# Residual turns of the out and down projection, from TensorE to VectorE's 32 x 32 blocks, in a hybrid decoder block on one core

## The chip, the cores and the metric

One Trainium2 chip, one of its cores. The metric is the device time of one execution in microseconds (us), taken over several runs. The profiled execution is one more run, with its own time; its span is the time from the first to the last instruction in the trace.

## What is computed

The block adds two residuals. The lines that matter here:

```python
h = jnp.concatenate([meta, x], axis=1)            # 16 meta tokens ahead of 256
...
m = (jax.nn.sigmoid(ga) * (y_h @ w_branch_hgrn[l])
     + jax.nn.sigmoid(gb) * (y_a @ w_branch_dsa[l]))
h = h + m @ w_out[l]                              # residual 1: x, 2048 channels
u = rmsnorm(h, ffn_norm_w[l])
a = causal_dwconv(u @ w_ffn_gate[l], ffn_conv_w[l], ffn_conv_b[l])
h = h + (jax.nn.silu(a) * (u @ w_ffn_up[l])) @ w_ffn_down[l]   # residual 2: h
return rmsnorm(h, final_norm_w)[:, N_META:]
```

x is float32, one sequence of 256 tokens, 2048 channels. The input x lies in memory with a token per row.

## The kernel before

Every weight matrix is cut into units of 128 columns, all 2048 rows (16 slices of 128). There are 256-column panels of raw float32 weights, two buffers, loaded by SyncE (`load`, L433); each panel waits for `lo_ready`, the low parts of the panel two before it. ScalarE rounds a unit to `w_hi` (L1136), VectorE makes the rest `w_lo` (L1447), both four units deep, and TensorE makes three products per slice: high by high, high by low, low by high. The order of the work on each engine is written out by hand, and engines meet at semaphores. `ahead(n)` on ScalarE and VectorE makes the high and low part of unit n + 3.

Through the gates, the merge (16 units from `U_MERGE`) and the out projection (16 units from `U_OUT`) activations lie turned: 128 channels on the partitions, tokens along the row. T is 272, TQ is 258: the last two meta tokens and the 256 of x. The unit n of the out projection gives channels 128n to 128n + 127 of h.

Residual 1. x has tokens on the rows, so TensorE turns it into the bank of the unit, ahead of the products (L1031: three turns of 128 x 128 a unit, one for the meta rows and two for x, with the identity), and the 48 products of the unit are summed on top. POOL fetches x for two units at a time into `x_st` (`x_panel`, L603 and L604), two buffers, the first two before its loop over the gates of the merge. VectorE then copies the bank to `h_res` (L1794, `out_free`), ScalarE makes the scaled and rounded `u2_hi` (L1385; the profile calls the place u_hi) and VectorE its rest `u2_lo` (L1796). TensorE may use one of the two banks (`ps[6]`, `ps[7]`) again when `out_free` tells that the unit two before has been copied. POOL sums the squares of h over the units (L626, L631). This stage is a loop of 4 x 4 units on all engines.

The feed-forward has two halves of 22 blocks of hidden channels (`FH`). Its first unit begins with eight slices, then TensorE sums the squares over the partitions (L1058 for the units up to 14, L1060 for the last), and ScalarE and VectorE make the root of it (`h_rs`).

Residual 2. The down projection gives tokens on the rows again. In half 0, `residual` (L1079) turns h back on TensorE, four turns of 128 x 128 ahead of each of the eight groups of sums (two chunks of columns, two halves of a chunk, two blocks of tokens), into the bank in which `down` sums the products (L1092 to L1095). VectorE copies the bank to `h_tok` (`add`, L1851), which has the place of `h_res`; in half 1 it adds (L1853).

## Time and profile before

| | |
|---|---|
| median of 3 runs | 1599.75 us (1599.56 to 1600.13) |
| profiled execution | 1599.79 us |
| its span | 1598.0 us |
| granted TensorE clock | 0.999 of full speed |
| TensorE busy | 1586.3 us, 99% of the span |
| VectorE busy | 972.0 us, 61% |
| ScalarE busy | 708.5 us, 44% |
| POOL busy | 116.0 us, 7% |
| moved by DMA | 290.36 MB, mean 182 GB/s |

The busy time is an average over all stages. A line number such as L1031 is a line of the kernel. "PE" is TensorE's matmul side, DVE is VectorE, ACT is ScalarE, SP is SyncE; "SPq" and "ACTq" are their queues of transfers. Matmuls are pipelined, so a row's duration is longer than the distance from one to the next; the starts tell the pace.

### The profile page before, as it was taken

The page shows a single profiled execution, that of the slowest core. Times are in us where ns is not written, and L with a number is a line of the kernel's source. Part 1 is how long each engine was busy: PE and PEld are TensorE (multiplying, and loading weights), DVE is VectorE, ACT ScalarE, POOL GpSimd, SP SyncE. Part 2 cuts the span into 40 slices and gives each one's busy share as a digit, 9 for nine tenths or more (in the row PEclk, how much of TensorE's full clock was granted, in tenths as well). Part 3 has the DMA queues.
Part 4 walks back from the last instruction along what each step waited for, and adds up shares of the span by engine and source line. Part 5 has one row for each costly group of instructions (what it writes and reads, how often), then busy time and mean ns, then how long its engine had stood idle before and what let it go on. Part 6 is the DMA issues. An engine that isn't in the chain of part 4 may idle for free.

```text
span 1598.0 us, 29335 instructions
## 1 busy us (share of the span) xinstructions
PE 1586.3 (99%) x12162; PEld 1527.7 (96%) x12162; DVE 972.0 (61%) x1126; ACT 708.5 (44%) x746; POOL 116.0 (7%) x165
## 2 busy tenths in 40 slices
PE   9999999999999999999999999999999999999998
PEld 8999999999999999999999999998889999999886
DVE  7655878853355566786656666665445666666453
ACT  6433554544443345654345455544333334334342
POOL 1000140000000002352220000000000000000000
PEclk9999999999999999999999999999999999999999
DMA  7755555555555553576555565645455555565551
GB/s 244 227 179 164 158 165 179 178 179 179 179 189 180 159 159 119 191 246 203 177 191 191 172 195 165 203 162 204 173 198 181 188 180 187 174 194 198 196 210 54
DMA packets 244998, 290.36 MB, mean 182 GB/s; under 512 B 5697, under 2 KB 231218, under 8 KB 244530
## 3 DMA queue, kind: packets, MB, share of 16 engines
q1 hardware_dynamic: 238146, 278.78, 53.4%
q0 software_dynamic: 2176, 6.34, 1.2%
q10 hardware_dynamic: 4608, 4.23, 0.8%
q8 instruction: 55, 0.90, 0.2%
q14 instruction: 13, 0.11, 0.0%
HBM read 283.02 MB, written 6.32 MB: 181 GB/s over the span
## 4 chain that ended last, share of the span: by engine, by line
PE 99%; DVE 0%; ACT 0%; DMA 0%; issue 0%; SPq 0%; DVEq 0%
PE ps L654 25%; PE ps L655 24%; PE ps L656 24%; PE ps L1092 5%; PE ps L1095 5%; PE ps L1094 5%; PE ps L1041 2%; PE ps L1039 2%; PE ps L1040 2%; PE ps L817 1%; PE ps L685 0%; PE ps L792 0%; PE ps L934 0%; PE ps L1031 0%; PE ps L827 0%; PE ps L1079 0%
## 5 line engine op out<-in xcount | busy, mean ns | idle before, releaser
L654 PE MATMUL ps<-u_hi,w_hi 128*128 128x258 f32 (+2 forms) x2936 | 839.1, 286 | 0.0
L655 PE MATMUL ps<-u_lo,w_hi 128*128 128x258 f32 (+2 forms) x2936 | 831.4, 283 | 0.0
L656 PE MATMUL ps<-u_hi,w_lo 128*128 128x258 f32 (+2 forms) x2936 | 831.1, 283 | 0.0
L1447 DVE TENSOR_TENSOR w_lo<-raw,w_hi 128x2048 fp32r<-128x2048 f32 x259 | 598.1, 2309 | 353.6 <-ACT w_hi L1136 353.1
L1136 ACT ACTIVATE w_hi<-raw 128x2048 fp32r<-128x2048 f32 x259 | 495.9, 1916 | 565.1 <-PE ps L656 393.4
L654 PEld LDWEIGHTS ps<-u_hi,w_hi 128*128 128x128 f32 x2936 | 554.0, 189 | 5.1 <-DVE z_qf L1560 2.5
L655 PEld LDWEIGHTS ps<-u_lo,w_hi 128*128 128x128 f32 x2936 | 554.0, 189 | 0.3
L656 PEld LDWEIGHTS ps<-u_hi,w_lo 128*128 128x128 f32 x2936 | 553.8, 189 | 0.0
L1092 PE MATMUL ps<-w_hi,hid_hi 128*128 128x512 f32 x352 | 137.8, 391 | 0.0
L1095 PE MATMUL ps<-w_lo,hid_hi 128*128 128x512 f32 x352 | 137.1, 389 | 0.0
L1094 PE MATMUL ps<-w_hi,hid_lo 128*128 128x512 f32 x352 | 137.0, 389 | 0.0
L1095 PEld LDWEIGHTS ps<-w_lo,hid_hi 128*128 128x128 f32 x352 | 66.1, 188 | 14.0
L1094 PEld LDWEIGHTS ps<-w_hi,hid_lo 128*128 128x128 f32 x352 | 66.1, 188 | 13.4
L1092 PEld LDWEIGHTS ps<-w_hi,hid_hi 128*128 128x128 f32 x352 | 66.1, 188 | 13.3
L1039 PE MATMUL ps<-m_hi,w_hi 128*128 128x258 f32 x256 | 73.7, 288 | 0.0
L1041 PE MATMUL ps<-m_hi,w_lo 128*128 128x258 f32 x256 | 72.7, 284 | 0.0
L1040 PE MATMUL ps<-m_lo,w_hi 128*128 128x258 f32 x256 | 72.3, 283 | 0.0
L1318 ACT ACTIVATE gate_st<-ps 128x258 f32<-128x258 f32 x32 | 12.4, 387 | 100.0 <-PE ps L656 100.0
L1040 PEld LDWEIGHTS ps<-m_lo,w_hi 128*128 128x128 f32 x256 | 48.6, 190 | 0.0
L1039 PEld LDWEIGHTS ps<-m_hi,w_hi 128*128 128x128 f32 x256 | 48.5, 189 | 0.0
L1041 PEld LDWEIGHTS ps<-m_hi,w_lo 128*128 128x128 f32 x256 | 48.4, 189 | 0.0
L1834 DVE TENSOR_TENSOR g_raw<-ps,h_rs 128x258 f32<-128x258 f32 x44 | 18.8, 428 | 39.6 <-PE ps L656 37.9
(299 smaller groups left out, 1307.4 us busy)
## 6 DMA issues: line engine op xcount, KB each, us to landing
raw<-in_w_in_dram SPq DMA_DIRECT2D x47, 2048.0 KB, 8.5
raw<-in_w_ffn_gate_dram SPq DMA_DIRECT2D x22, 2048.0 KB, 8.1
raw<-in_w_ffn_up_dram SPq DMA_DIRECT2D x22, 2048.0 KB, 8.1
raw<-in_w_ffn_down_dram SPq DMA_DIRECT2D x20, 2048.0 KB, 7.6
raw<-in_w_out_dram SPq DMA_DIRECT2D x8, 2048.0 KB, 8.9
raw<-in_w_branch_hgrn_dram SPq DMA_DIRECT2D x8, 1024.0 KB, 5.5
raw<-in_w_branch_dsa_dram SPq DMA_DIRECT2D x8, 1024.0 KB, 8.8
gate_spill<-gate_st ACTq DMA_DIRECT2D x32, 129.0 KB, 3.9
```

The costliest lines, as they stand in the source:

```text
L654: mm(acc, w_hi[s][:, k, :], mov_hi(k), start=(k == first), stop=False)
L655: mm(acc, w_hi[s][:, k, :], mov_lo(k), start=False, stop=False)
L656: ins = mm(acc, w_lo[s][:, k, :], mov_hi(k), start=False, stop=(k == last))
L1039: mm(acc, w_hi[n % 4][:, k, :], m_hi[:, k, :], start=False, stop=False, skip_group_check=True)
L1040: mm(acc, w_hi[n % 4][:, k, :], m_lo[:, k, :], start=False, stop=False, skip_group_check=True)
L1041: ins = mm(acc, w_lo[n % 4][:, k, :], m_hi[:, k, :], start=False, stop=(k == KT - 1), skip_group_check=True)
L1092: mm(acc, hid_hi[:, f, rows], down_hi[s][:, i, :], start=(f == 0 and half == 1), stop=False, skip_group_check=True)
L1094: mm(acc, hid_lo[:, f, rows], down_hi[s][:, i, :], start=False, stop=False, skip_group_check=True)
L1095: ins = mm(acc, hid_hi[:, f, rows], down_lo[s][:, i, :], start=False, stop=(f == FH - 1), skip_group_check=True)
L1136: activation(w_hi[m % 4][:], raw[(m // 2) % 2][:, :, P * (m % 2):P * (m % 2) + P], ACT.Copy)\
L1447: v.tensor_tensor(w_lo[m % 4][:], raw[(m // 2) % 2][:, :, P * (m % 2):P * (m % 2) + P], w_hi[m % 4][:].bitcast(F32), ALU.subtract).then_in ...
L1834: link(v.tensor_tensor(g[:], ps[4 * half + u][:, 0:TQ], h_rs[:], ALU.mult))
```

## The change

TensorE turns nothing in the two projections any more.

x now comes from memory already shuffled: `x_blocks` views it in blocks of 32 tokens by 32 channels, and POOL's `x_quad` moves the channels of four units with 16 transfers of 32 partitions x 8 blocks x 32 numbers (128 bytes a piece) into `x_sh`, two buffers. A turn of VectorE within blocks of 32 x 32 (L1811) then gives `xt` with channels on the partitions. The meta rows are fetched by four more transfers and turned once, for all units (`xm_sh`, `xm`). VectorE turns x for a unit before it waits for that unit's products, adds bank and `xt` instead of copying the bank, turns h into `h_sh` behind `u2_lo`, and ScalarE stores `h_sh` with four transfers of 128-byte pieces to `h_spill` in memory, one unit later. When all is stored, POOL reads h back with tokens on the rows into `h_tok`, two transfers of 1 MB, and half 0 of the down projection adds to it, as half 1 does. The start flags of the sums change with that. The stage is written out flat on VectorE, ScalarE and POOL, no longer a loop.

```diff
--- before.py
+++ after.py
@@ -188,7 +188,11 @@
 
         HRES = R[0] + 2 * FH * SEQ * 4
         h_res = at("h_res", HRES, [P, KT, TQ])
-        x_st = [at(f"x_st{a}", BIAS + 3072 * a, [P, 3, 256]) for a in range(2)]
+        x_sh = [at(f"x_sh{a}", (BIAS, R[4])[a], [P, 4, SEQ]) for a in range(2)]
+        xt = [at(f"xt{a}", BIAS + 4096 + 1024 * a, [P, SEQ]) for a in range(2)]
+        xm_sh = at("xm_sh", R[7] + 5184, [P, KT, 32])
+        xm = at("xm", R[4] + 4096, [P, KT, 32])
+        h_sh = [at(f"h_sh{a}", R[4] + 6144 + 1024 * a, [P, SEQ]) for a in range(4)]
         h_sq = at("h_sq", R[7] + 640, [P, TQ])
         ssq = at("ssq", R[7] + 1672, [P, TQ])
         h_rs = at("h_rs", R[7] + 2704, [P, TQ])
@@ -374,6 +385,9 @@
         bd_cols = w_branch_dsa[0].rearrange("(k p) n -> p k n", p=P)
         wd_rows = w_ffn_down[0].rearrange("(k p) n -> p k n", p=P)
         x_rows = x[0].rearrange("(t p) n -> p t n", p=P)
+        x_blocks = x[0].rearrange("(b j) (k a i) -> a j k b i", j=32, a=4, i=32)
+        meta_blocks = meta_tokens.rearrange("j (k a i) -> a j k i", a=4, i=32)
+        h_blocks = h_spill.rearrange("(b j) (k a i) -> a j k b i", j=32, a=4, i=32)
 
 
         N_PANELS = U_END // 2
@@ -599,17 +613,8 @@
             pool.wait_ge(x_rs_ready, 1)
             for n in range(4):
                 gate_pair(n, n)
-            def x_panel(slot, cols):
-                pool.dma_start(x_st[slot][:, 1:3, :], x_rows[:, :, cols]).then_inc(x_st_in[slot], 16)
-                pool.dma_start(x_st[slot][P - 2:P, 0, :], meta_tokens[T0:META, cols]).then_inc(x_st_in[slot], 16)
-
             for n in range(3):
                 scale_gates(n, 16)
-            pool.wait_ge(o_gated, HEADS)
-            steps.link(pool, pool.memset(ssq[:], 0.0))
-            for b in range(2):
-                steps.link(pool, pool.memset(x_st[b][:, 0, :], 0.0))
-                x_panel(b, slice(256 * b, 256 * b + 256))
             with pool.Fori(0, 3) as i:
                 for a in range(4):
                     pool.wait_ge(m_ready, 4 * i + (a + 1))
@@ -619,6 +624,12 @@
                     scale_gates((a + 3) % 4, 16 * i + (16 if a == 0 else 32))
             scale_gates(3, 64)
 
+
+            def x_quad(q):
+                for a in range(4):
+                    for k in range(4):
+                        pool.dma_start(x_sh[q % 2][32 * a:32 * a + 32, k, :].rearrange("j (b i) -> j b i", i=32),
+                                       x_blocks[a, :, 4 * q + k, :, :]).then_inc(x_sh_in[q % 2], 16)
 
             def squares(n, tile, last=False):
                 pool.wait_ge(out_free, n + 3)
@@ -630,18 +641,32 @@
                     steps.link(pool, ins)
                     steps.link(pool, pool.tensor_tensor(ssq[:], ssq[:], h_sq[:], ALU.add))
 
-            with pool.Fori(0, 3) as i:
-                steps.enter(i, 8)
-                for b in range(2):
-                    pool.wait_ge(xt_turned, 4 * i + (2 * b + 2))
-                    x_panel(b, ds(512 * i + (512 + 256 * b), 256))
-                    for a in range(2):
-                        squares(4 * i + (2 * b + a), ds(4 * i + (2 * b + a), 1))
-            steps.leave(3)
-            for n in range(12, 16):
+            pool.wait_ge(o_gated, HEADS)
+            steps.link(pool, pool.memset(ssq[:], 0.0))
+            pool.wait_ge(projected, U_MERGE)
+            pool.wait_ge(ya_ready, 9)
+            pool.memset(xm_sh[:], 0.0).then_inc(xm_zeroed, 1)
+            x_quad(0)
+            pool.wait_ge(xm_zeroed, 1)
+            for a in range(4):
+                pool.dma_start(xm_sh[32 * a:32 * a + 2, :, :], meta_blocks[a, T0:META, :, :]).then_inc(xm_in, 16)
+            pool.wait_ge(projected, U_OUT)
+            x_quad(1)
+            for n in range(16):
+                if n in (4, 8):
+                    pool.wait_ge(xt_turned, n)
+                    x_quad(n // 4 + 1)
                 if n == 15:
                     pool.tensor_copy(spare[:, 5:6], ssq[:, 0:1]).then_inc(ssq_ready, 1)
                 squares(n, slice(n, n + 1), n == 15)
+            pool.wait_ge(u2h_ready, 16)
+            pool.wait_ge(u2l_ready, 16)
+            for a in range(4):
+                pool.wait_ge(h_out[a], 4 * 64)
+            pool.wait_ge(ssq_ready, 2)
+            for c in range(2):
+                pool.dma_start(h_tok[c][:], h_spill[:, 1024 * c:1024 * c + 1024].rearrange("(t p) n -> p t n", p=P))\
+                    .then_inc(h_in, 16)
 
 
         @block.tensor
@@ -1023,23 +1048,13 @@
             with pe.Fori(0, 4) as i:
                 for u in range(4):
                     n = U_OUT + u
-                    if u % 2 == 0:
-                        pe.wait_ge(x_st_in[u // 2], 32 * i + 32)
                     pe.wait_ge(out_free, 4 * i + (u + 1))
-                    bank = ps[6 + u % 2]
-                    for t in range(3):
-                        ins = mm(bank[:, P * t:P * t + P], x_st[u // 2][:, t, P * (u % 2):P * (u % 2) + P], ident[:],
-                                 is_transpose=True, start=(t == 0), stop=False, skip_group_check=True)
-                    ins.then_inc(xt_turned, 1)
                     pe.wait_ge(lo_ready, 4 * i + (n + 1))
                     for k in range(KT):
                         if u == 0 and k >= 14:
                             pe.wait_ge(m_ready, k + 1)
-                        acc = bank[:, P - 2:P - 2 + TQ]
-                        mm(acc, w_hi[n % 4][:, k, :], m_hi[:, k, :], start=False, stop=False, skip_group_check=True)
-                        mm(acc, w_hi[n % 4][:, k, :], m_lo[:, k, :], start=False, stop=False, skip_group_check=True)
-                        ins = mm(acc, w_lo[n % 4][:, k, :], m_hi[:, k, :], start=False, stop=(k == KT - 1),
-                                 skip_group_check=True)
+                        ins = products(ps[6 + u % 2][:, 0:TQ], n % 4, (k,), lambda k: m_hi[:, k, :],
+                                       lambda k: m_lo[:, k, :])
                     ins.then_inc(projected, 1)
             for half, (u_ff, u_down) in enumerate(((U_FF, U_DOWN), (U_FF2, U_DOWN2))):
 
@@ -1073,23 +1088,14 @@
                         gate_up(u, range(KT))
 
 
-                def residual(c, u, t):
-
-                    for g in range(4):
-                        mm(ps[down_bank(0, c, u, t)][:, P * g:P * g + P],
-                           h_res[:, 8 * c + 2 * g + u, 2 + P * t:2 + P * t + P], ident[:], is_transpose=True,
-                           start=(g == 0), stop=False, skip_group_check=True)
-
                 def down(j, t, half=half, u_down=u_down):
 
                     s = (u_down + j) % 4
                     for i in range(4):
                         c, f = down_at(j, i)
-                        if f == 0 and half == 0:
-                            residual(c, j % 2, t)
                         acc = ps[down_bank(half, c, j % 2, t)][:]
                         rows = slice(P * t, P * t + P)
-                        mm(acc, hid_hi[:, f, rows], down_hi[s][:, i, :], start=(f == 0 and half == 1), stop=False,
+                        mm(acc, hid_hi[:, f, rows], down_hi[s][:, i, :], start=(f == 0), stop=False,
                            skip_group_check=True)
                         mm(acc, hid_lo[:, f, rows], down_hi[s][:, i, :], start=False, stop=False, skip_group_check=True)
                         ins = mm(acc, hid_hi[:, f, rows], down_lo[s][:, i, :], start=False, stop=(f == FH - 1),
@@ -1380,14 +1386,21 @@
             loop(U_MERGE, 4, 4, merge_unit, early=1)
 
 
-            def out_unit(i, u, split):
-                act.wait_ge(out_free, 4 * i + (u + 3))
-                activation(u2_hi[:, ds(4 * i + u, 1), :].rearrange("p a t -> p (a t)"),
-                           h_res[:, ds(4 * i + u, 1), :].rearrange("p a t -> p (a t)"), ACT.Copy,
-                           scale=vec_a[:, ds(4 * i + (V_FFN + u), 1)]).then_inc(u2h_ready, 1)
-                split()
-
-            loop(U_OUT, 4, 4, out_unit, early=1)
+            def store_turned(u):
+                act.wait_ge(h_turned, u + 1)
+                for a in range(4):
+                    act.dma_start(h_blocks[a, :, u, :, :],
+                                  h_sh[u % 4][32 * a:32 * a + 32, :].rearrange("j (b i) -> j b i", i=32))\
+                        .then_inc(h_out[u % 4], 16)
+
+            for u in range(16):
+                act.wait_ge(out_free, u + 3)
+                activation(u2_hi[:, u, :], h_res[:, u, :], ACT.Copy, scale=vec_a[:, V_FFN + u:V_FFN + u + 1])\
+                    .then_inc(u2h_ready, 1)
+                ahead(U_OUT + u + 1)
+                if u:
+                    store_turned(u - 1)
+            store_turned(15)
             act.wait_ge(ssq_sum, 1)
             activation(h_rs[:], ps[4][:, 0:TQ], ACT.Sqrt, bias=eps[:], scale=1.0 / D).then_inc(h_std, 1)
 
@@ -1786,18 +1799,27 @@
                         .then_inc(m_ready, 1)
 
 
-            with dve.Fori(0, 4) as i:
-                for u in range(4):
-                    m = U_OUT + u
-                    dve.wait_ge(projected, 4 * i + (m + 1))
-                    h = h_res[:, ds(4 * i + u, 1), :].rearrange("p a t -> p (a t)")
-                    v.tensor_copy(h, ps[6 + u % 2][:, P - 2:P - 2 + TQ]).then_inc(out_free, 1)
-                    dve.wait_ge(u2h_ready, 4 * i + (u + 1))
-                    v.scalar_tensor_tensor(u2_lo[:, ds(4 * i + u, 1), :].rearrange("p a t -> p (a t)"), h,
-                                           vec_a[:, ds(4 * i + (V_FFN + u), 1)],
-                                           u2_hi[:, ds(4 * i + u, 1), :].rearrange("p a t -> p (a t)").bitcast(F32),
-                                           ALU.mult, ALU.subtract).then_inc(u2l_ready, 1)
-                    ahead(4 * i + (m + 1), m + 1)
+            for u in range(16):
+                m, h = U_OUT + u, h_res[:, u, :]
+                if u == 0:
+                    dve.wait_ge(xm_in, 64)
+                    v.transpose(xm[:].rearrange("p k t -> p (k t)"), xm_sh[:].rearrange("p k t -> p (k t)"))\
+                        .then_inc(xm_turned, 1)
+                    dve.wait_ge(xm_turned, 1)
+                if u % 4 == 0:
+                    dve.wait_ge(x_sh_in[(u // 4) % 2], 256 * (u // 8) + 256)
+                v.transpose(xt[u % 2][:], x_sh[(u // 4) % 2][:, u % 4, :]).then_inc(xt_turned, 1)
+                dve.wait_ge(xt_turned, u + 1)
+                dve.wait_ge(projected, m + 1)
+                v.tensor_tensor(h[:, 0:2], ps[6 + u % 2][:, 0:2], xm[:, u, 0:2], ALU.add)
+                v.tensor_tensor(h[:, 2:TQ], ps[6 + u % 2][:, 2:TQ], xt[u % 2][:], ALU.add).then_inc(out_free, 1)
+                dve.wait_ge(u2h_ready, u + 1)
+                v.scalar_tensor_tensor(u2_lo[:, u, :], h, vec_a[:, V_FFN + u:V_FFN + u + 1], u2_hi[:, u, :].bitcast(F32),
+                                       ALU.mult, ALU.subtract).then_inc(u2l_ready, 1)
+                if u >= 4:
+                    dve.wait_ge(h_out[u % 4], 64 * (u // 4))
+                v.transpose(h_sh[u % 4][:], h[:, 2:TQ]).then_inc(h_turned, 1)
+                ahead(m + 1, m + 1)
 
 
             dve.wait_ge(h_std, 1)
@@ -1820,6 +1842,9 @@
                     for u in range(4):
                         m = u_ff + u
                         if u == 3:
+                            if half == 0:
+                                for r in range(4):
+                                    dve.wait_ge(h_out[r], 4 * 64)
                             low(0)
                         if u >= 2:
                             c = conv[u - 2][:]
@@ -1843,14 +1868,14 @@
                     low(1)
                 steps.leave(FH // 2)
 
+                if half == 0:
+                    dve.wait_ge(h_in, 32)
+
                 def add(c, u, t, half=half):
 
                     h = chunk_cols(c, t, u)
                     bank = ps[down_bank(half, c, u, t)][:].rearrange("p (g c) -> p g c", c=P)
-                    if half == 0:
-                        v.tensor_copy(h, bank).then_inc(down_added, 1)
-                    else:
-                        v.tensor_tensor(h, bank, h, ALU.add).then_inc(down_added, 1)
+                    v.tensor_tensor(h, bank, h, ALU.add).then_inc(down_added, 1)
 
                 for j in range(1, FH - 3):
                     ahead(u_down + j, u_down + j)
```

POOL, at the end of its loop over the merge gates and into the out projection, before (x_st is the staged x, h_sq the squares, ssq their sum):

```order
L594 TENSOR_TENSOR gates_125<-gates_125,x_rs 128x516
L633 UNCONDITIONAL_BRANCH
L633 ISA
L603 ISA
L603 DMA x_st_127<-in_x_dram 128x2x256
L604 ISA
L604 DMA x_st_127<-in_meta_tokens_dram 2x256
L624 REGISTER_ALU
L626 ISA
L626 TENSOR_TENSOR h_sq<-h_res 128x258
```

The same place of POOL in the change:

```order
L608 TENSOR_TENSOR gates_125<-gates_125,x_rs 128x516
L645 MEMSET ssq 128x258
L648 MEMSET xm_sh 128x512
L631 DMA x_sh_127<-in_x_dram 32x8x32 x16
L652 DMA xm_sh<-in_meta_tokens_dram 2x16x32 x4
L631 DMA x_sh_128<-in_x_dram 32x8x32 x16
L637 TENSOR_TENSOR h_sq<-h_res 128x258
L642 TENSOR_TENSOR ssq<-ssq,h_sq 128x258
```

The first fetch of x has moved from ahead of the gate loop to behind it, and 36 transfers stand there where 2 stood; two more runs of 16 stand behind the squares of units 3 and 7.

VectorE, from the last unit of the merge into the first of the out projection, before:

```order
L1447 TENSOR_TENSOR w_lo_56<-raw_49,w_hi_52 128x2048
L1784 ISA
L1784 TENSOR_TENSOR m_lo<-gates_125,m_hi 128x258
...
L1794 COPY h_res<-ps 128x258
L1795 REGISTER_ALU
L1796 ISA
L1796 SCALAR_TENSOR_TENSOR u_lo<-h_res,vec_a,u_hi 128x258
L1446 REGISTER_ALU
L1447 TENSOR_TENSOR w_lo_57<-raw_50,w_hi_53 128x2048
```

And in the change:

```order
L1460 TENSOR_TENSOR w_lo_56<-raw_49,w_hi_52 128x2048
L1797 ISA
L1797 TENSOR_TENSOR m_lo<-gates_125,m_hi 128x258
...
L1806 STREAM_TRANSPOSE xm<-xm_sh 128x512
L1811 STREAM_TRANSPOSE xt_129<-x_sh_127 128x256
L1814 TENSOR_TENSOR h_res<-ps,xm 128x2
L1815 TENSOR_TENSOR h_res<-ps,xt_129 128x256
L1817 SCALAR_TENSOR_TENSOR u_lo<-h_res,vec_a,u_hi 128x258
L1821 STREAM_TRANSPOSE h_sh_133<-h_res 128x256
L1460 TENSOR_TENSOR w_lo_57<-raw_50,w_hi_53 128x2048
```

Two turns and a small add have come into each unit, one turn ahead of the wait for the products and one ahead of `w_lo`, and the turn of the meta rows once; the register work of the loop is gone.

## Rows read from the trace of the kernel before

**Rows 1.** The page: the chain that ended last, shares of the span by engine
```profile
PE 99%; DVE 0%; ACT 0%; DMA 0%; issue 0%; SPq 0%; DVEq 0%
```

**Rows 2.** TensorE's timeline between two out-projection units: start us, us, engine, line, op
```profile
780.40 0.28 PE L1041 MATMUL ps<-m_hi,w_lo 128*128 128x258 f32 x1
780.52 0.49 PE L1031 MATMUL ps<-ident,x_st 128*128 128x128 f32 x3
780.97 0.29 PE L1040 MATMUL ps<-m_lo,w_hi 128*128 128x258 f32 x1
```

**Rows 3.** Line L1031: its turns, ns min/median/max, first and last start
```profile
L1031 PE MATMUL ps<-ident,x_st x48: 270/272/273, 743.8 to 835.8; 128*128 128x128 f32 x48
```

**Rows 4.** Timeline of TensorE at the turns of h in the down projection
```profile
1157.90 0.40 PE L1095 MATMUL ps<-w_lo,hid_hi 128*128 128x512 f32 x1
...
1158.59 0.39 PE L1095 MATMUL ps<-w_lo,hid_hi 128*128 128x512 f32 x1
...
1159.72 0.40 PE L1095 MATMUL ps<-w_lo,hid_hi 128*128 128x512 f32 x1
```

**Rows 5.** Timeline of VectorE and ScalarE, one unit of the out projection
```profile
774.72 0.43 DVE L1794 COPY h_res<-ps 128x258 f32 x1 [0.82 <-PE ps L1041]
...
775.37 0.51 ACT L1385 ACTIVATE u_hi<-h_res,vec_a  x1 [3.80 <-DVE h_res L1794]
775.79 1.90 ACT L1136 ACTIVATE w_hi<-raw 128x2048 fp32r<-128x2048 f32 x1
...
777.73 2.66 DVE L1447 TENSOR_TENSOR w_lo<-raw,w_hi 128x2048 fp32r<-128x2048 f32 x1 [1.19 <-ACT w_hi L1136]
```

**Rows 6.** Groups of VectorE: line, op, count, busy us, mean ns, idle before
```profile
L1853 DVE TENSOR_TENSOR h_tok<-ps,h_tok 128x512 f32<-128x512 f32 x8 | 5.3, 687 | 12.6 <-PE ps L1095 12.6
...
L1804 DVE RECIPROCAL h_rs<-h_rs 128x258 f32<-128x258 f32 x1 | 1.8, 1759 | 0.0
```

**Rows 7.** Timeline of VectorE and ScalarE in code written out flat
```profile
652.88 0.77 DVE L1761 TENSOR_TENSOR z_v<-z_v,z_g 128x258 f32<-128x258 f32 x2 [1.37 <-ACT z_g L1364]
...
653.34 0.42 ACT L1367 ACTIVATE yh_hi<-z_v 128x258 fp32r<-128x258 f32 x1 [0.26 <-DVE z_v L1761]
```

**Rows 8.** A transfer's issue on ScalarE's queue, line L1320: ns min/median/max
```profile
L1320 ACTq DMA_DIRECT2D gate_spill<-gate_st x32: 338/338/383, 227.2 to 434.6; - x32
```

**Rows 9.** Timeline of VectorE and POOL ahead of the out projection
```profile
660.23 2.29 DVE L1447 TENSOR_TENSOR w_lo<-raw,w_hi 128x2048 fp32r<-128x2048 f32 x1 [1.38 <-ACT w_hi L1136]
...
660.88 0.76 POOL L603 DMA_DIRECT2D x_st<-in_x_dram  x1 [0.30 <-POOL x_st L611]
...
733.19 1.20 POOL L594 TENSOR_TENSOR gates<-gates,x_rs 128x516 f32<-128x516 f32 x1 [4.74 <-DMA gates<-gate_spill]
```

**Rows 10.** Lines L603 and L604, POOL's transfers: ns min/median/max, landing of L604
```profile
L603 POOL DMA_DIRECT2D x_st<-in_x_dram x8: 745/788/791, 659.0 to 812.3; - x8
...
L604 POOL DMA_DIRECT2D x_st<-in_meta_tokens_dram x8: 534/534/546, 659.7 to 813.1; - x8
...
DMA to landing us min/median/max: 2.6/5.9/7.0
```

**Rows 11.** DMA: out projection (share is 0.58), first 14 us, page's queues
```profile
743.80:841.50 97.70, 97.70 (x817) 97.70 (x816) 57.82 (x50) 37.02 (x32) 27.13 (x43) 1.00 0.58 186
...
DMA packets 3434, 3.91 MB, mean 279 GB/s; under 512 B 2150, under 2 KB 3162, under 8 KB 3162
...
q1 hardware_dynamic: 3434, 3.91, 86.2%
...
q1 hardware_dynamic: 238146, 278.78, 53.4%
...
q10 hardware_dynamic: 4608, 4.23, 0.8%
```

**Rows 12.** Timeline of POOL and TensorE at the sum of squares
```profile
842.55 0.62 POOL L626 TENSOR_TENSOR h_sq<-h_res 128x258 f32<-128x258 f32 x1 [4.39 <-DVE h_res L1794]
...
845.03 0.60 PE L1060 MATMUL ps<-h_sq,ones 128*128 128x258 f32 x2
```

More of the change, by code:

```diff
@@ L223, in hybrid_block @@
         gate_spill = nc.dram_tensor("gate_spill", (P, 2 * KT, TQ), F32).ap()
+        h_spill = nc.dram_tensor("h_spill", (SEQ, D), F32).ap()
         def sem(name):
@@ L339, in hybrid_block @@
         m_ready = sem("m_ready")
-        x_st_in = [sem("x_st_in0"), sem("x_st_in1")]
+        x_sh_in = [sem("x_sh_in0"), sem("x_sh_in1")]
+        xm_zeroed = sem("xm_zeroed")
+        xm_in = sem("xm_in")
+        xm_turned = sem("xm_turned")
         xt_turned = sem("xt_turned")
+        h_turned = sem("h_turned")
+        h_out = [sem(f"h_out{a}") for a in range(4)]
+        h_in = sem("h_in")
         ssq_ready = sem("ssq_ready")
```

## The prediction

> **What bounds the kernel now.** I read the page's chain of waits first: TensorE is 99% of the chain that ended last [rows 1]. So an edit pays only by what it takes off TensorE's instruction stream, and costs only by what makes TensorE wait. Two questions follow: how much do the 80 turns on TensorE (L1031, 48; L1079, 32) really take there, and does any new feeder become late. For the first I read TensorE's timeline around one turn of each kind [rows 2 to 4], for the second the loop that VectorE and ScalarE run beside each unit of the out projection [rows 5 to 8], POOL's queue [rows 9, 10] and the DMA engines [rows 11].
>
> **What leaves TensorE.** The busy time of a turn (272 ns [rows 3]) overstates it, since matmuls are pipelined; the starts tell. In the out projection a turn of three starts 0.12 us after the product before it, as any product does, but the second product behind it starts 0.45 us after the turn (780.52 to 780.97), where two products would start 0.12 apart: 0.33 us per unit [rows 2]. 16 units: **5.3 us**. In the down projection the third product of a group starts 1.13 us after the one before the turns (1158.59 to 1159.72), where three products behind each other take 0.69 us (1157.90 to 1158.59): 0.44 us per group of four, 8 groups: **3.5 us** [rows 4]. Nothing takes their place on TensorE, so 8.8 us is the most that can be won. The down part I take in full: its h is read back right behind the out projection, at about 850 us, and VectorE first adds it some 300 us later (at L1851's place), and the add that replaces the copy reads the same 512 columns from the bank, 0.69 us as in half 1 [rows 6]. The eight adds of half 0 cost nothing.
>
> **VectorE's loop in the out projection.** Before, a unit of TensorE lasts 6.12 us (15 units from 743.8 to 835.8, less the two turns between, 0.15) [rows 3]; after, 5.79. VectorE, ScalarE and VectorE form a ring per unit: copy of h, u_hi on ScalarE, w_hi on ScalarE, w_lo on VectorE, next copy [rows 5]. Its gaps: w_hi 0.42 behind u_hi, w_lo 1.94 behind w_hi, 2.29 for w_lo alone [rows 9]. From the copy's start to u_hi it is 0.65 in this looped code, but 0.46 in code written out flat (z_v 652.88, yh_hi 653.34) [rows 7], and the change writes this stage out flat. The change adds to the ring: the two-column add (258 columns cost 0.43 and 512 cost 0.69, so the fixed part is 0.17 at most; 0.1, as it runs behind another) and the turn of x ahead of the wait. No row shows a VectorE turn. Its lower bound is a copy of that width, 0.42 us; its upper the dearest row of that width, the reciprocal, 1.76 us; I take 0.42, since it too passes each column once, plus 0.05 for its own semaphore [rows 5, 6]. Ring: 0.1 + 0.46 + 0.42 + 1.94 + 2.29 + 0.47 = **5.7 us**, just under the 5.79 of TensorE. The second turn (h) fits in the 1.2 us for which VectorE waits for w_hi. ScalarE's four stores a unit are 4 x 0.34 = 1.4 us, beside 3.80 us that it idles before u_hi; what is queued behind them, the next u_hi, is not due before that [rows 5, 8].
>
> **The start of the stage.** VectorE now waits for the meta rows and the first x quad before it may free the first bank. POOL reaches them after its last gate product (733.19 + 1.20); two memsets, then 16 transfers at 0.79 (the nearest row: 256 pieces as well, 0.788) and 4 meta transfers at 0.55: 735.3 + 12.6 + 2.2 = 750.1. These landed 2.6 to 7.0 us after issue, 5.9 in the median, which I take: most of those eight had a weight load beside them, and so has this one [rows 9, 10]. Landed 756.0; turn of 512 columns 0.69, turn of x 0.47, adds 0.55: the first bank is free at 757.8. TensorE needs it at 743.8 + 2 x 5.79 = 755.4, and so waits **2.5 us**. From there VectorE is one unit further behind than before, and its ring (5.7) barely gains on TensorE (5.79).
>
> **The end of the stage.** The feed-forward begins with 24 products (0.12 each, 2.87 us), then a first product for the sum of squares (0.43 us from the one start to the other) and a second, for which POOL must have squared the last h (it ended at 843.17; L1060 starts at 845.03, so it was no wait) [rows 12]. After: TensorE could be there at 757.9 + 14 x 5.79 + 2.87 + 0.43 = 842.3. VectorE's last add ends at 757.8 + 15 x 5.68 = 843.0, POOL's square and a hop make 843.8. L1060 starts at 843.8, **1.2 us** earlier than before: of 5.3 us, 2.6 go at the start (the wait and a hop of 0.1) and 1.5 at the end. **Sum:** 1.2 + 3.5 = 4.7 us. The profiled execution took 1599.79, the median of the runs is 1599.75; 1599.8 - 4.7 = **1595.1 us**.
>
> **The small packets.** x and h now move in pieces of 128 bytes: three quads (12288) and the stores (16384) within the stage, 1792 packets per DMA engine. The engines are busy 0.58 of 97.7 us of the stage, 56.7 us; TensorE's 16 units are 92.6 us, so a packet may cost 20 ns before the engines are full. Bounds: in the first 14 us 3434 packets took 0.862 x 14 x 16 = 193 us; 2150 were under 512 bytes, and the other 3.25 MB at the kernel's mean (13.65 ms for 278.78 MB) are 159 us, leaving 16 ns for a small one. The upper end is the mean packet, 57 ns (1.2 KB), and the nearest store, 44 ns (q10: 0.8% of 16 x 1598 us for 4608 packets) [rows 11]. I take 16, as the nearest in size: 28.7 us, engines 92% full, and free of charge, though with little to spare.
>
> **Rivals.**
> 1. *No wait at the start* (meta lands in 2.6 us, the bank frees at 754.5): VectorE never limits TensorE and all 8.8 us stay: 1591.0. Against it: a weight load runs beside it. Chance 0.10.
> 2. *The ring is longer than a unit.* If the VectorE turn costs 0.8, or POOL's products catch w_lo (2.29 becomes 2.66 at 777.73, and in every second unit before [rows 5]), the ring is 5.9 to 6.1; each 0.1 us is 1.5 us at L1060. 1598 to 1603. Chance 0.13.
> 3. *The DMA engines fill up: slower.* Place: the 128-byte stores of ScalarE's queue beside the weight loads. It decides from 20 ns a packet. At 44 ns for a store the stage needs 56.7 + 12.3 + 45.1 = 114 us of every engine, 21.5 over the 92.6: 1599.8 - 8.8 + 21.5 = 1612.5; with 57 ns for all, 1657. For it: the margin is thin, and a late store also holds VectorE, which waits for the stores of four units ago before it turns h. Against it: the 16 ns above. Chance 0.17. The Trainium skill, "DMA: Bandwidth & Descriptors", Specifications, says that below 512 B the engine does read-modify-write; by that rule this case would hold, while the rows show small reads only and no small store.
> 4. *POOL's queue is late: slower.* Place: x_quad, 64 transfers in all. Each 0.1 us above 0.79 is 1.6 us at the start, and from 1.37 us a transfer quads 2 and 3 miss their units too. At 2 us: 1599.8 - 8.8 + 2.5 + 19.4 + 2 x 10 = 1633. For it: 16 in a row are in no row. Against: a transfer issued inside a w_lo (660.88 within 660.23 to 662.52) took its normal 0.76, w_lo its normal 2.29 [rows 9]. The Trainium skill, "SBUF — State Buffer", SBUF: two separate sides, warns that VectorE in a two-port mode locks GpSimd out of writing descriptors; by it, with two w_lo in the way, the queue would be 4.6 us late at the start, 1600 in all; this row of the trace disagrees, for w_lo at least. Chance 0.14.
> My own case has 0.46, its range is 1592.5 to 1599.
>
> **How the numbers follow.** 0.2% (3.2 us) is about what a measurement of this kernel can tell from no change, so faster means under 1596.6. Faster: two thirds of my case (0.31), rival 1 (0.10), a little of the others: 0.42. Same: the rest of my case and most of rival 2, a little of 3 and 4: 0.25. Slower: 0.33, nearly all of rivals 3 and 4. The range runs from the 1591 of rival 1 to 1616, which takes in rival 2 and the lower half of 3 and 4.
>
> **What would show it.** No L1031 and L1079 rows; TensorE's unit at 5.8 us; one wait of 2 to 3 us at the third unit, on VectorE's add, and one of 1 to 2 us at the sum of squares. A VectorE turn of 256 columns near 0.42, x_quad transfers near 0.79, small packets near 16 ns with a DMA share of 0.9 in the stage. Wrong if TensorE waits for lo_ready (late weights: rival 3), if VectorE waits for the x quads at units 4, 8 or 12 (rival 4), or if the down projection shortens by other than 3.5 us.

## The result and the profile after

The change takes 1590.11 us (median of 6 runs, 1589.83 to 1590.3) against 1599.71 us before (6 runs, 1599.56 to 1600.13): ratio 0.9939, 95% interval 0.9929 to 0.9950, so 9.6 us less. Its profiled span is 1588.5 us, 9.5 below the 1598.0 of before. The direction was forecast; the gain is twice the 4.7 us of the sum and ends just outside the range, whose low end was 1591.0.

TensorE's timeline where the two stages begin and end gives the whole of it. First the timeline of the change:

```profile
743.95 0.28 PE L679 MATMUL ps<-m_hi,w_hi 128*128 128x258 f32 x1
...
836.12 0.28 PE L679 MATMUL ps<-u_hi,w_hi 128*128 128x258 f32 x1
...
839.43 0.60 PE L1075 MATMUL ps<-h_sq,ones 128*128 128x258 f32 x2
...
1089.12 0.39 PE L1098 MATMUL ps<-w_hi,hid_hi 128*128 128x512 f32 x1
...
1208.58 0.39 PE L1101 MATMUL ps<-w_lo,hid_hi 128*128 128x512 f32 x1
```

and of the kernel before, at the same places:

```profile
743.84 0.49 PE L1031 MATMUL ps<-ident,x_st 128*128 128x128 f32 x3
...
841.73 0.28 PE L654 MATMUL ps<-u_hi,w_hi 128*128 128x258 f32 x1
...
1094.73 0.60 PE L1079 MATMUL ps<-ident,h_res 128*128 128x128 f32 x4
...
1218.05 0.39 PE L1095 MATMUL ps<-w_lo,hid_hi 128*128 128x512 f32 x1
```

The out projection takes 836.12 - 743.95 = 92.17 us instead of 97.89: 5.7 less. From there to the first down product it is 253.0 us in both. The down projection takes 119.46 us between the rows instead of 123.32: 3.9 less. 5.7 + 3.9 = 9.6. TensorE waits for nothing between 740 and 860 us, and L1075 follows the out projection by 3.31 us, as L1060 did before (845.03 - 841.73 = 3.30, [rows 12]).

What was to be late is on POOL and VectorE. POOL's timeline ahead of the stage, in the change (start us, us, engine, line, op, count):

```profile
732.92 1.20 POOL L608 TENSOR_TENSOR gates<-gates,x_rs 128x516 f32<-128x516 f32 x1 [4.36 <-DMA gates<-gate_spill]
...
734.91 9.24 POOL L631 DMA_DIRECT2D x_sh<-in_x_dram  x16
744.15 2.39 POOL L652 DMA_DIRECT2D xm_sh<-in_meta_tokens_dram  x4
```

The 16 transfers of the first x quad take 9.24 us, 0.58 each. The view of these lines (ns min/median/max, then from issue to landing):

```profile
L631 POOL DMA_DIRECT2D x_sh<-in_x_dram x64: 582/582/630, 734.9 to 802.4; - x64
...
DMA to landing us min/median/max: 1.9/5.7/7.0
```

VectorE's timeline of the first unit and the start of the second:

```profile
750.80 0.71 DVE L1806 STREAM_TRANSPOSE xm<-xm_sh 128x512 f32<-128x512 f32 x1 [2.08 <-DMA xm_sh<-in_meta_tokens_dram]
751.54 0.45 DVE L1811 STREAM_TRANSPOSE xt<-x_sh 128x256 f32<-128x256 f32 x1
752.02 0.16 DVE L1814 TENSOR_TENSOR h_res<-ps,xm 128x2 f32<-128x2 f32 x1
752.10 0.41 DVE L1815 TENSOR_TENSOR h_res<-ps,xt 128x256 f32<-128x256 f32 x1
...
753.50 0.44 DVE L1821 STREAM_TRANSPOSE h_sh<-h_res 128x256 f32<-128x256 f32 x1
754.90 2.29 DVE L1460 TENSOR_TENSOR w_lo<-raw,w_hi 128x2048 fp32r<-128x2048 f32 x1 [0.96 <-ACT w_hi L1142]
757.11 0.44 DVE L1811 STREAM_TRANSPOSE xt<-x_sh 128x256 f32<-128x256 f32 x1
757.58 0.16 DVE L1814 TENSOR_TENSOR h_res<-ps,xm 128x2 f32<-128x2 f32 x1
757.66 0.41 DVE L1815 TENSOR_TENSOR h_res<-ps,xt 128x256 f32<-128x256 f32 x1
```

and ScalarE's, between:

```profile
752.55 0.51 ACT L1398 ACTIVATE u_hi<-h_res,vec_a 128x258 fp32r<-128x258 f32 x1 [6.18 <-DVE h_res L1815]
752.97 1.90 ACT L1142 ACTIVATE w_hi<-raw 128x2048 fp32r<-128x2048 f32 x1
```

VectorE does wait for the meta rows (2.08 us), but the first bank is free at 752.10 + 0.41 = 752.5, and TensorE wants it at 743.95 + 2 x 5.76 = 755.5. The ring (757.66 - 752.10) is 5.56 us, TensorE's unit 92.17 / 16 = 5.76. A turn of 256 columns takes 0.44 us, one of 512 columns 0.71.

Twelve of the fifteen rings are 5.56 or 5.57 us, the last is 5.61, and two are 6.01 us. In these two `w_lo` begins 0.05 us after POOL has begun an addition to `ssq`, and takes 2.75 us instead of 2.29 (POOL's row, then VectorE's; the other pair is at 805.4):

```profile
782.66 0.64 POOL L642 TENSOR_TENSOR ssq<-ssq,h_sq 128x258 f32<-128x258 f32 x1
782.71 2.75 DVE L1460 TENSOR_TENSOR w_lo<-raw,w_hi 128x2048 fp32r<-128x2048 f32 x1 [0.96 <-ACT w_hi L1142]
```

So VectorE's mean is (836.47 - 752.10) / 15 = 5.62 us, 0.14 less than TensorE's unit, and not 0.20.

The DMA engines, out projection of the change: windows (start:end, length, busy us of PE, PEld, DVE, ACT, POOL, granted clock, DMA share, GB/s), then the queues over the whole stage (packets, MB, share of 16 engines):

```profile
743.80:755.80 12.00, 12.00 (x102) 12.00 (x101) 7.21 (x12) 4.54 (x4) 11.98 (x22) 1.00 1.07 240
755.80:767.80 12.00, 12.00 (x102) 12.00 (x101) 9.06 (x13) 4.64 (x4) 5.17 (x6) 1.00 0.65 174
767.80:792.20 24.40, 24.40 (x205) 24.40 (x204) 17.75 (x28) 9.55 (x9) 14.86 (x25) 1.00 0.90 238
792.20:836.30 44.10, 44.10 (x370) 44.10 (x369) 31.82 (x46) 18.28 (x16) 20.11 (x33) 1.00 0.77 221
```

```profile
q1 hardware_dynamic: 16448, 16.71, 58.5%
q10 hardware_dynamic: 14354, 1.73, 12.6%
q0 software_dynamic: 1977, 1.91, 11.2%
```

The engines are at their fullest in the first 12 us, when two x quads land beside weights, and TensorE still waits for nothing. A store's packet costs 12.6% x 92.18 us x 16 / 14354 = 12.9 ns.

### The profile page after: what moved, and what is told of

Its sections match the earlier page's. It is cut to its first block, busy times and chain, and to the rows that moved or that the text cites. A ratio compares the mean times of both kernels' runs of the same rounds, so it can differ in the third digit from the quotient of the medians.

```text
span 1588.5 us, 29146 instructions
## 1 busy us (share of the span) xinstructions
PE 1576.7 (99%) x12082; PEld 1518.4 (96%) x12082; DVE 978.4 (62%) x1175; ACT 708.4 (45%) x746; POOL 144.8 (9%) x218
## 3 DMA queue, kind: packets, MB, share of 16 engines
q1 hardware_dynamic: 238146, 278.78, 53.9%
## 4 chain that ended last, share of the span: by engine, by line
PE 99%; DVE 0%; ACT 0%; DMA 0%; issue 0%; SPq 0%; DVEq 0%
PE ps L679 27%; PE ps L680 26%; PE ps L681 26%; PE ps L1101 5%; PE ps L1100 5%; PE ps L1098 5%; PE ps L842 1%; PE ps L710 0%; PE ps L817 0%; PE ps L959 0%; PE ps L852 0%; PE ps L995 0%; PE ps L950 0%; PE ps L906 0%; PE ps L956 0%; DMA x_tok<-in_meta_tokens_dram 0%
```

## Experiments

The theory after the result, T: TensorE gets back exactly what its turns took; VectorE's ring and POOL's queue have a slack of 0.2 us a unit and 2.9 us at the start (3.0 by the rows above), so nothing they do is seen; the two small margins of the prediction are real, only nearer than it said. The rival S: some of the 9.6 us comes from elsewhere (weights that come in another order, the flat code), and the new feeders cost something under it.

**1. No residual at all.** The kernel before, without its 80 turns and with nothing in their place: its output lacks both residuals.

```diff
-                    for t in range(3):
-                        ins = mm(bank[:, P * t:P * t + P], x_st[u // 2][...], ident[:], is_transpose=True, ...)
...
-                        if f == 0 and half == 0:
-                            residual(c, j % 2, t)
```

> The kernel before, with the 80 turns of the two residuals taken off TensorE and nothing put in their place (x and h are not added: the output lacks both residuals; all transfers, copies and loops stay). Theory T, that the change wins exactly what the turns took and all its new work is free: the same time as the change, 1590.1 us, out projection 92.2 us and down projection of half 0 119.7 us. Rival S, that part of the 0.8 us above my sum of 8.8 comes from the flat code or the gone copies and not from the turns: 1590.9 us, with a unit of 5.79 us.

Measured: 1590.31 us (1590.15 to 1590.34), ratio 0.9940 (0.9926 to 0.9954), span 1588.4; the out projection again 92.17 us. The kernel that only drops the turns and the one that does their work elsewhere take the same time: the gain is the turns, the feeders cost nothing, and S falls.

**2 and 3. One half of the change each.** The change with the down projection's residual left on TensorE (`residual` back, no `h_sh`, no stores), and the change with x left on TensorE (`x_panel` and L1031's turns back).

```diff
+                        if f == 0 and half == 0:
+                            residual(c, j % 2, t)
...
-                v.transpose(h_sh[u % 4][:], h[:, 2:TQ]).then_inc(h_turned, 1)
...
-                    store_turned(u - 1)
```

> The change for residual 1 only: x from VectorE's turns, h stays in place, the 32 turns of residual 2 are back on TensorE, no stores and no reload of h. T: the out projection takes 92.2 us, the down projection 123.6 us, the whole 1590.1 + 3.9 = 1594.0 us. If the stores of h cost TensorE something in the out projection, the stage gets shorter than 92.2 us.

```diff
+                    for t in range(3):
+                        ins = mm(bank[:, P * t:P * t + P], x_st[u // 2][...], ident[:], is_transpose=True, ...)
...
-                v.transpose(xt[u % 2][:], x_sh[(u // 4) % 2][:, u % 4, :]).then_inc(xt_turned, 1)
...
+                v.tensor_copy(h, ps[6 + u % 2][:, P - 2:P - 2 + TQ]).then_inc(out_free, 1)
```

> The change for residual 2 only: h turned by VectorE, stored and reloaded; x is turned on TensorE as before, from x_st. T: out projection 97.9 us, down projection 119.7 us, the whole 1599.7 - 3.9 = 1595.8 us. Rival S (flat code shortens the units): out projection under 97.5 us and 1595.3 us.

Measured: out part alone 1594.18 us (ratio 0.9965, 0.9951 to 0.9979), span 1592.3; down part alone 1596.43 (ratio 0.9977, 0.9968 to 0.9987), span 1594.8. In the first the out projection is 92.17 us, with or without the stores of h; in the second it is 97.89 as before, though the code is flat, with the down projection 3.9 us shorter. So the flat code gives nothing by itself. The parts are 5.7 and 3.2 us of span. In the second TensorE also reached the stage 0.3 us later than before (744.14), and what follows its last product took 8.5 us instead of the 8.2 of the change: both lie outside the stages that were edited, and why they differ is not shown. They add up to the whole, within that.

**4, 5 and 6. The first quad later.** The change with 9, 17 and then 6 more fills of `xm_sh` on POOL ahead of `x_quad(0)`. They write the zeros that are there anyway, and take only POOL's time, 0.58 us each.

```diff
+            for _ in range(9):
+                steps.link(pool, pool.memset(xm_sh[:], 0.0))
             pool.memset(xm_sh[:], 0.0).then_inc(xm_zeroed, 1)
             x_quad(0)
```

> The change with nine more memsets on POOL ahead of the first x quad, some 5.4 us, which puts the first freed bank where the prediction had it (757.8). T, with the ring of 5.57 us that the trace of the change shows: TensorE waits 2.5 us at the third unit, the ring then gains 0.19 us a unit and there is no second wait at the sum of squares: 1592.6 us. The prediction's own ring of 5.68 us: a second wait of 1.5 us, 1594.1 us. If TensorE's wait is no matter of this bank: 1590.1 us.

> As before with 17 memsets, some 10.2 us. T: bank free at 762.7, TensorE waits 7.3 us at the third unit and 0.3 us at the sum of squares: 1597.7 us. With the ring of 5.68: 1.9 us at the sum, 1599.3 us.

> The change, with 6 more fills ahead of the first x_quad on POOL's queue instead of 9 or 17, so that the first bank comes free near 757.9 us, where the prediction had put it. TensorE should wait 2.3 to 2.5 us at the third unit. If a wait of that length leaves the granted clock alone, as the waits of 1.4 and 2.4 us at the end of the stage with x turned twice did, the time is near 1592.5 us. If the clock falls as it did after the wait of 5.3 us, 1.9 us come on top: near 1594.4 us. The prediction's own sum, with its turns of 8.8 us and a wait at the end as well, gives 1595.1 us.

Measured: with 9 fills 1596.93 us (1595.21 to 1598.39; ratio 0.9982, 0.9973 to 0.9992), with 17 fills 1600.47 (ratio 1.0005, 0.9996 to 1.0015): both dearer than expected (1592.6 and 1597.7). With 6 fills 1593.61 (1593.26 to 1594.88; ratio 0.9963, 0.9949 to 0.9977), between the 1592.5 and 1594.4 of the two cases written down.

The run with 9 fills missed its aim. The quad began at 740.98, 6.1 us later than in the change instead of 5.4, and the meta rows landed 6.3 us after their last issue instead of 4.3: the first bank was free at 760.7, not 757.8. With 17 fills it was free at 762.9 (762.7 expected).

VectorE's and TensorE's timelines with 9 fills:

```profile
758.95 0.71 DVE L1808 STREAM_TRANSPOSE xm<-xm_sh 128x512 f32<-128x512 f32 x1 [10.32 <-DMA xm_sh<-in_meta_tokens_dram]
```

```profile
760.80 0.58 PE L681 MATMUL ps<-m_hi,w_hi 128*128 128x258 f32 x1 [5.25 <-DVE h_res L1817]
761.18 0.42 PE L682 MATMUL ps<-m_lo,w_hi 128*128 128x258 f32 x1
761.39 0.42 PE L683 MATMUL ps<-m_hi,w_lo 128*128 128x258 f32 x1
```

and with 6:

```profile
757.69 0.38 PE L681 MATMUL ps<-m_hi,w_hi 128*128 128x258 f32 x1 [2.06 <-DVE h_res L1817]
757.90 0.28 PE L682 MATMUL ps<-m_lo,w_hi 128*128 128x258 f32 x1
758.02 0.29 PE L683 MATMUL ps<-m_hi,w_lo 128*128 128x258 f32 x1
...
842.76 0.70 PE L1077 MATMUL ps<-h_sq,ones 128*128 128x258 f32 x2 [0.86 <-POOL h_sq L637]
```

TensorE waits for the first bank at its third unit, as the prediction described. After a wait of 5.25 us its products start 0.21 us apart instead of 0.12, until 764.6; after one of 2.06 us they start 0.21 apart once and then 0.12. The granted clock (the third number from the end) in windows of the kernel with 9 fills, then of the one with 17:

```profile
757.00:757.50 0.50, 0.00 (x0) 0.00 (x0) 0.00 (x0) 0.00 (x0) 0.50 (x2) 1.00 1.02 222
757.50:758.00 0.50, 0.00 (x0) 0.00 (x0) 0.00 (x0) 0.00 (x0) 0.50 (x2) 0.79 1.12 254
758.00:758.50 0.50, 0.00 (x0) 0.00 (x0) 0.00 (x0) 0.00 (x0) 0.50 (x2) 0.50 1.08 166
764.50:765.00 0.50, 0.50 (x6) 0.50 (x6) 0.50 (x1) 0.00 (x0) 0.00 (x0) 0.88 0.00 0
```

```profile
761.00:767.00 6.00, 3.98 (x18) 3.99 (x19) 4.51 (x7) 2.31 (x2) 5.99 (x10) 0.50 0.32 55
767.00:773.00 6.00, 6.00 (x47) 6.00 (x46) 4.65 (x7) 2.32 (x2) 3.00 (x4) 0.89 0.13 22
```

0.50 is the lower of TensorE's two levels, 1.2 instead of 2.4 GHz. With 9 fills the clock fell inside the wait, at about 757.8, 2.2 us after TensorE's last product had ended, and rose at 764.6, after 3.8 us of work; with 17 fills it fell at about 758.1, 2.8 us into the wait, and rose at 768.3, after 5.3 us of work. The stage is 99.37 us with 9 fills and 102.57 with 17: 7.2 and 10.4 over the 92.17, of which the waits are 5.3 and 7.8 and the clock the other 1.9 and 2.6, half of the 3.8 and 5.3 us. That is what the expectations lacked, beside the late quad of the 9 fills.

With 6 fills the first bank is free at 757.6, where the prediction had put it. TensorE then loses 2.3 us in the stage (94.50 us) and 1.0 at the sum of squares (L1077 starts 4.33 us behind the stage's end, not 3.31): both waits of the prediction, at their places, 3.3 us together where it had 4.0. With 9 fills there is no wait at the end, since TensorE, slowed by its clock, gets there after POOL. So the ring does set the end once the start is late. But it does so by two rings only: as in the change, two of the fifteen are 6.02 us, with a `w_lo` of 2.75 that begins 0.04 us after POOL's `ssq`. Without these 0.9 us VectorE's last add would have ended at 841.1 instead of 842.0, and nearly all of the 1.0 us at the end would be gone. The slowest of the five executions (1594.88, no trace) had a mean granted clock of 0.997 and the others 0.998 or 0.999, so in that one the clock may have fallen.

**7. Stores twice.** Each of ScalarE's stores is issued twice, the second to another place in memory.

```diff
-                    act.dma_start(h_blocks[a, :, u, :, :], ...)
+                    for blocks in (h_blocks, h_blocks2):
+                        act.dma_start(blocks[a, :, u, :, :], ...)
```

> The change with every store of h sent twice, to two places in memory: 16384 more packets of 128 bytes in the stage. By the 13.5 ns that such a packet took in the change's trace the 16 DMA engines go from 77 to 92 us of the 92 us of the stage: T says full, but no wait over 1 us, 1590.1 to 1591.1 us. Rival 3 of the prediction (a small store holds the engines for longer than its packet shows, so weights come late): 1595 us or more, with TensorE waiting on lo_ready.

Measured: 1590.92 us (1590.5 to 1592.57), ratio 0.9947 (0.9931 to 0.9964), span 1588.8; TensorE waits nowhere in the stage. The queue of the stores over the stage, and the windows after the first 24 us:

```profile
q10 hardware_dynamic: 28288, 3.41, 24.4%
```

```profile
767.80:792.20 24.40, 24.40 (x206) 24.40 (x205) 16.62 (x25) 9.28 (x8) 14.47 (x24) 1.00 1.02 254
792.20:836.30 44.10, 44.10 (x369) 44.10 (x369) 31.02 (x49) 18.54 (x16) 20.05 (x33) 1.00 0.89 231
```

Twice the packets take twice the share, 24.4% x 92.18 us x 16 / 28288 = 12.7 ns each, and the engines are full for 24 us without TensorE noticing. Rival 3 falls: even twice the stores fit. The margin is not much more than that, and it is lost at another place than the rival's. ScalarE's issues of stores took up to 2.3 us each while the engines were full, and its `u_hi` at 787.94 came late behind them, so that one ring of VectorE is 7.24 us and the last add comes 1.8 us later against TensorE than in the change. POOL's last square then ends at 839.55, just ahead of the product that needs it (839.61), and the first down product comes 0.09 us later. The median is 0.8 us above the change's and one of the four runs 2.5 us (1592.57, no trace).

**8. A longer ring.** The turn of x is done twice.

```diff
+                link(v.transpose(xt[u % 2][:], x_sh[(u // 4) % 2][:, u % 4, :]))
                 v.transpose(xt[u % 2][:], x_sh[(u // 4) % 2][:, u % 4, :]).then_inc(xt_turned, 1)
```

> The change with the turn of x done twice in each unit, so that VectorE's ring is 6.05 us instead of 5.57, longer than TensorE's unit of 5.76. T: the first bank is free at 753.0; from the eleventh unit TensorE waits 0.3 us a unit for a bank, then 1.3 us for the low part of u2 and 2.4 us at the sum of squares: the sum of squares comes 5.1 us later, 1595.2 us. If a long ring is absorbed by the four units of weights in advance: 1590.1 us.

Measured: 1595.86 us (1594.67 to 1598.57), ratio 0.9977 (0.9966 to 0.9988), span 1595.1. VectorE's timeline of one unit, and TensorE's waits (total us, times, longest):

```profile
802.47 0.41 DVE L1816 TENSOR_TENSOR h_res<-ps,xt 128x256 f32<-128x256 f32 x1
...
808.50 0.41 DVE L1816 TENSOR_TENSOR h_res<-ps,xt 128x256 f32<-128x256 f32 x1
```

```profile
PE ps L1075 <- POOL h_sq L637: 2.0, 1, 2.0
PE ps L679 <- DVE u_lo L1818: 1.1, 1, 1.1
```

The ring is now 6.03 us, 0.27 over TensorE's unit. From its sixth unit on TensorE has the same pace, as two of its units show; its waits there are short (0.28 us where products start 0.12 apart) and the view of waits does not list them:

```profile
803.01 0.38 PE L679 MATMUL ps<-m_hi,w_hi 128*128 128x258 f32 x1
...
809.04 0.38 PE L679 MATMUL ps<-m_hi,w_hi 128*128 128x258 f32 x1
```

The stage takes 96.50 us, 4.3 more: 3.0 in these units and the rest at the first product of the feed-forward (the wait of 1.1). The sum of squares takes 2.3 more (the wait of 2.0), and the first down product comes 2.4 us later against the stage's end. The expectation had the waits begin at the eleventh unit. They began earlier since the first bank was free at 754.5, 0.8 us before it is needed and not 3.0: 0.5 for the second turn and 1.5 for the landing of the meta rows, 5.8 us here. By the medians one more turn of 0.47 us, which a ring with that much slack would hide, costs 5.8 us: the slack of the ring is really only 0.1 to 0.2 us a unit.

**9. The first quad earlier.** `x_quad(0)` and the meta transfers are issued before POOL's loop of gates in the merge instead of behind it.

```diff
+            x_quad(0)
+            pool.wait_ge(xm_zeroed, 1)
+            for a in range(4):
+                pool.dma_start(xm_sh[...], meta_blocks[...]).then_inc(xm_in, 16)
             with pool.Fori(0, 3) as i:
...
-            x_quad(0)
```

> The change, with x_quad of the first unit and its meta transfers issued ahead of POOL's gates of the merge instead of behind them. If nothing waits at the start of the change (the first bank free at 752.5 us, needed at 755.4), an earlier start brings nothing: 1590.1 us, and only more slack. The other way: the 20 issues, 11.7 us of POOL's queue, hold up the gates, VectorE's merge waits for them, and the stage starts later: slower by up to some 10 us.

Measured: 1591.63 us (1591.6 to 1591.67), ratio 0.9948 (0.9932 to 0.9965), span 1590.0, 1.5 over the change. The out projection is 92.17 us again, so an earlier quad gives nothing, but it begins 1.5 us later. POOL's timeline in the merge shows why:

```profile
658.84 9.25 POOL L619 DMA_DIRECT2D x_sh<-in_x_dram  x16
668.07 2.39 POOL L632 DMA_DIRECT2D xm_sh<-in_meta_tokens_dram  x4
670.46 0.75 POOL L636 DMA_DIRECT2D gates<-gate_spill  x1
```

The first gate transfer starts at 670.46 instead of 667.43, and TensorE waits for VectorE's gates twice, 2.2 us, where it waited once, 0.9. The mechanism is that of the other case, at a seventh of its bound. The change's own place for the quad is the better one, and no kernel tried beats the change.

## Why the prediction was off

The sum had 4.7 us of gain: 8.8 us of turns less 4.1 of waits. Measured are 9.6 us and no wait. So some 4 us of the miss are waits that did not occur, and 0.8 are the turns.

**The bound: right.** TensorE is 99% of the chain in both, and the time fell by what left its stream, as experiment 1 shows on its own.

**What leaves TensorE: mis-sized, by 0.8 us.** The prediction had 0.33 us per unit and 0.44 per group; the stages give 5.72 / 16 = 0.36 and 3.86 / 8 = 0.48. The readings stopped at the second and third product behind the turns, and the loss goes on growing behind them. Set product by product beside the change, the stream of before is 0.33 us late at the second product behind the three turns of x, 0.34 at the fourth and 0.36 from the twenty-third on (means of 15 units); behind the first four turns of h it is 0.44 late at the second and 0.46 at the seventh, and it has lost 0.48 a group over the eight. Why the products behind a turn come a little late is not shown. The stage's length over its count, before and with plain 0.12 us products, would have given 97.89 - 16 x 48 x 0.12 = 5.7 at once.

**The start of the stage: the step that failed.** It had the first bank free at 757.8, 2.4 after it is needed; it was free at 752.5, 3.0 before. Of the 5.3 us, 3.4 are the price of an x_quad transfer, taken as 0.79 from [rows 10] because both have 256 pieces, and 0.58 in truth. The transfer of [rows 10] spans 128 partitions and this one 32. 1.6 are the landing behind the last issue, 4.3 us instead of the median 5.9. The other 0.3 are small: POOL began 0.4 earlier, the meta issues were 0.2 longer, and VectorE's part, 1.7 us as its terms said (0.69 + 0.47 + 0.55), had been added up as 1.8. The landing of 4.3 us is the luck of one execution: it was 4.8 with 17 fills, 5.5 with 6 and 6.3 with 9 (experiments 5, 6 and 4), and 5.8 in experiment 8, where POOL's issues stand at the same times as in the change. So 5.9 was no bad number, and the issue price is what decided: even after the 5.8 us of experiment 8 the bank, less its second turn, would have been free at 754.1, in time. Both ends of the landing, 2.6 and 7.0, were in the prediction's rows; of the issue price it gave no lower end. With 0.58 alone the prediction's bank would have been free at 754.4, in time even with the 5.9.

**VectorE's ring: nearly right, and it mattered.** 5.68 was forecast, 5.56 is measured in most units and 5.62 in the mean. The turn (0.44, and 0.47 from start to start), the add to u_hi (0.45 in flat code for 0.46) and w_hi's gaps came as predicted. The 0.08 is `w_lo`, 2.29 busy but 2.21 to the next start, the same trap as with the turns: a row's duration is not its pitch. The rest is rounding and the two-column add, 0.08 for 0.1. The price of a store's issue on ScalarE's queue was too low: 0.34 was taken, and the median of 64 is 0.47 us, the longest 1.33. It cost nothing, since ScalarE still idles 3.2 us before `u_hi`.

**The end: right in kind, absent in fact.** With the bank at 757.6 (experiment 6) both waits appear, 2.3 and 1.0 us for 2.5 and 1.5. With the turns at their measured 9.6 and its own waits of 4.0 the prediction would have said 1594.2; with the measured waits it is 1599.8 - 9.6 + 3.3 = 1593.5, and 1593.61 was measured. That the end is near its forecast is in part luck, since it rests on the two long rings, which the forecast did not have.

**Small packets: right, with more room.** 12.9 ns for 16. The share of the stage is 0.82, not 0.92. The 56.7 us of before included the 4.9% of the stage (4.8 us) that the queue of POOL's transfers had there, all of it for the x transfers that the change removes. Of each engine's time the stores took 11.6 us (12.6%) in the stage instead of 16.4 and the x pieces 10.3 (11.2%) instead of 12.3, while the weights took 53.9 instead of 51.9. The profile counts the x pieces in larger packets (1977 with 1.91 MB), so there is no price of one of them.

**The rivals.** Rival 1 is what happened, at a chance of 0.10 that rested on landing time only: the cheaper issue, which leads to the same place, was in none of the cases. Rivals 3 and 4 did not occur: packets 12.9 ns, transfers 0.58. Of rival 2 one half did: POOL's products caught `w_lo` twice, 2.75 for 2.29, and made two rings of 6.01; the start that was 3.0 us early took them up, and TensorE saw nothing. Rival 4's warning by the Trainium skill, "SBUF — State Buffer", SBUF: two separate sides, that VectorE can lock GpSimd out of writing descriptors, is not seen beside `w_lo`, which ran twice meanwhile: the 16 issues of 734.91 to 744.15 took 0.58 each, like the other 48 (582 to 630 ns). What other operations of VectorE would do, no run here shows. Rival 3's rule, the same skill's "DMA: Bandwidth & Descriptors", Specifications, read-modify-write below 512 B, no run here shows at work or not; no store of 128 bytes was dear for it. The range ended at 1591.0 because it took the 8.8 us as exact; 24 times a reading that was 0.03 to 0.04 us short is 0.8, and an allowance of 1 us for it would have held the result.

## What to carry to other kernels

An idle engine can take a bound engine's work for nothing as long as its ring is shorter than the bound engine's unit, in the mean and with the instructions that another engine stretches: here 5.62 against 5.76 us, and one more instruction of 0.47 us cost 5.8. Price a transfer's issue from a row of like shape, in partitions as well as in pieces, and give every unknown a lower end, since a start that is safe by 3 us and one that is late by 2 were two prices apart. Measure what a kind of instruction costs by the length of a stage over its count, and by the start of one row to the start of the next, not by the busy time.

## Not expected of the hardware

- In waits of 5.25 and 7.8 us TensorE's granted clock fell to half, 2.2 and 2.8 us after its last product had ended. It rose again after 3.8 and 5.3 us of work (products 0.21 us apart until then), and that cost 1.9 and 2.6 us on top of the waits. In waits of 2.06 us, and of 1.1 and 2.0 us close together (1.36 and 2.41 from one product's start to the next), it did not fall. Waits of other lengths have no trace, and executions of one kernel differ: with 9 fills nine of ten had a mean granted clock of 0.996 or 0.997, and the fastest (1595.21) 0.999.
- `w_lo` (VectorE) took 2.75 us instead of 2.29 when it began 0.03 to 0.05 us behind POOL's addition to `ssq`, in both cases of the change and again in experiments 4 and 6. The other way round, POOL's `h_sq` that began inside a `w_lo` (755.75) took 1.91 us instead of 0.62.
- POOL's issue of a transfer took 0.58 us for 32 partitions and 0.75 to 0.79 for 128, though 256 pieces each. For two partitions it took 0.53 to 0.55 with one piece each, and 0.59 to 0.63 with 16 pieces each, no less than for 32 partitions. So neither count alone sets it; no experiment varied them.
- VectorE's turn in blocks of 32 costs about what a copy or an add of the width does, in single precision: 0.44 us for 256 columns beside a copy of 0.43, and 0.71 for 512 beside an add of 0.69.
